# Head sums of four query and key tiles side by side, one inversion for four, and roots copied back over the heads' partitions on ScalarE's queue

## The reference

```python
def rmsnorm(x, g):                     # x: (..., heads, 64)
    x32 = x.astype(jnp.float32)
    y = x32 * lax.rsqrt(jnp.mean(x32 * x32, axis=-1, keepdims=True) + EPS)
    return (y * g.astype(jnp.float32)).astype(x.dtype)

def apply_rope(x, cos, sin):
    half = HEAD_DIM // 2
    x1, x2 = x[..., :half], x[..., half:]
    return jnp.concatenate([x1 * c - x2 * s, x2 * c + x1 * s], axis=-1)

q = apply_rope(rmsnorm(p_q.reshape(B, n, n_heads, HEAD_DIM), qg), *rope)
k = apply_rope(rmsnorm(p_k.reshape(B, n, n_kv,    HEAD_DIM), kg), *rope)
...
o = softmax(q k^T / 8, masks, sinks) v
```

## Time and profile before

| | |
|---|---|
| three runs, median (lowest, highest) | 3043.26 us (3042.82, 3045.39) |
| the profiled execution, its own time | 3041.93 us |
| its span, first to last instruction | 3039.8 us |
| TensorE matmuls busy | 2926.5 us, 96% |
| VectorE busy | 1115.6 us, 37% |
| ScalarE busy | 622.8 us, 20% |
| mean granted TensorE clock | 0.994 |

### The profile page before, as it was taken

One profiled execution on the slowest core, in us unless ns is written; L12 is line 12 of the kernel. 1 busy time (PEld: TensorE's weight loads), 2 busy tenths in 40 slices (PEclk: granted clock), 3 DMA queues, 4 the chain that ended last, 5 costly groups with the idle time before them and its releaser, 6 DMA issues.

```text
span 3039.8 us, 33448 instructions
## 1 busy us (share of the span) xinstructions
PE 2926.5 (96%) x13265; PEld 1464.3 (48%) x13265; DVE 1115.6 (37%) x1678; ACT 622.8 (20%) x1157; POOL 78.3 (3%) x92
## 2 busy tenths in 40 slices
PE   7999999999999999999999999999979998999999
PEld 4565655555555222222234655677433333334547
DVE  4764546566614000000147554334121110138352
ACT  3145530000002110101022453111011101021161
POOL 1000000000000001102000000000000000000000
PEclk9999999999999999999999999999989999999999
DMA  8230013443523899999971201223489999974300
GB/s 256 66 94 15 15 38 129 174 165 125 165 78 111 355 374 396 368 401 349 364 208 38 80 28 30 74 83 90 180 337 417 418 418 418 418 227 114 83 1 28
DMA packets 252321, 587.50 MB, mean 193 GB/s; under 512 B 64280, under 2 KB 143912, under 8 KB 231048
## 3 DMA queue, kind: packets, MB, share of 16 engines
q1 hardware_dynamic: 237072, 554.02, 49.4%
q0 software_dynamic: 7680, 22.62, 2.5%
q10 hardware_dynamic: 7416, 8.71, 1.2%
HBM read 561.44 MB, written 15.21 MB: 190 GB/s over the span
## 4 chain that ended last, share of the span: by engine, by line
PE 87%; DMA 7%; DVE 3%; issue 1%; ACT 1%; SPq 1%; ACTq 0%; DVEq 0%; POOL 0%; POOLq 0%
PE ps L1076 26%; PE ps L1527 10%; PE ps L1651 7%; PE ps L1539 5%; PE ps L1141 5%; PE ps L1096 5%; PE ps L1191 5%; PE ps L1367 3%; PE ps L1355 3%; PE ps L1401 3%; PE ps L1204 2%; PE ps L1588 2%; PE ps L1165 2%; DMA ring<-in_w_e_up 1%; DMA ring<-in_w_e_down 1%; PE ps L1341 1%
## 5 line engine op out<-in xcount | busy, mean ns | idle before, releaser
L1076 PE MATMUL ps<-hT,ring 128*128 128x512 f32 (+1 forms) x1696 | 604.5, 514 | 3.5 <-ACT hT L1889 3.4
L1076 PEld LDWEIGHTS ps<-hT,ring 128*128 128x128 f32 x1696 | 321.9, 191 | 276.0 <-issue 251.9
L1527 PE MATMUL ps<-ring,hT 128*64 128x512 f32 x992 | 235.9, 605 | 3.0 <-DMA ring<-in_w_e_up 3.0
L1141 PE MATMUL ps<-hT,ring 128*128 128x512 f32 (+1 forms) x448 | 181.5, 533 | 0.7 <-DVEq L1874 0.7
L1651 PE MATMUL ps<-ring,hT 128*64 128x512 f32 x640 | 157.6, 602 | 17.4 <-DMA ring<-in_w_e_down 10.0
L1889 ACT ACTIVATE prob<-prob,nms 128x768 f32<-128x768 f32 (+5 forms) x224 | 159.2, 711 | 14.9 <-DVE nms L2582 4.5
L1191 PE MATMUL ps<-merged,ring 128*128 128x512 f32 (+1 forms) x384 | 142.7, 526 | 3.1 <-issue 3.1
L1367 PE MATMUL ps<-con,prob 128*128 128x128 f32 x872 | 140.1, 283 | 3.5 <-DVE merged L2606 1.6
L1076 PE MATMUL ps<-obuf,ring 128*128 128x512 f32 (+1 forms) x384 | 142.1, 523 | 0.0
L1367 PEld LDWEIGHTS ps<-con,prob 128*128 128x128 f32 x872 | 96.4, 140 | 91.8 <-issue 78.8
L1889 ACT ACTIVATE prob<-ps 128x768 f32<-128x768 f32 (+2 forms) x55 | 36.7, 667 | 490.7 <-PE ps L1076 418.9
(11 more groups left out here) (368 smaller groups left out, 3675.1 us busy)
## 6 DMA issues: line engine op xcount, KB each, us to landing
ring<-in_w_e_gate SPq DMA_DIRECT2D x79, 1024.0 KB, 15.4
ring<-in_w_e_up SPq DMA_DIRECT2D x65, 1024.0 KB, 14.4
ring<-in_w_e_down SPq DMA_DIRECT2D x60, 1024.0 KB, 13.5
ring<-in_w_in SPq DMA_DIRECT2D x49, 1024.0 KB, 6.1
ring<-in_w_ada SPq DMA_DIRECT2D x48, 1024.0 KB, 6.7
merged<-in_w_e_up SPq DMA_DIRECT2D x25, 1024.0 KB, 14.8
merged<-in_w_e_down SPq DMA_DIRECT2D x19, 1024.0 KB, 12.6
merged<-in_w_e_gate SPq DMA_DIRECT2D x18, 1024.0 KB, 16.0
```

What stands on the lines that cost most here:

```text
L1076: mm = pe.matmul(ps[:, b + a:b + e], lhs[:, k, :], rhs[:, k, a:e], start=k == 0, stop=k == nk - 1)
L1141: mm = pe.matmul(ps[:, BANK[SIDE]:BANK[SIDE] + hi - lo], ring3(slot)[:, k, m % 2 * P:(m % 2 + 1) * P], h3[:, k, lo:hi], start=k == 0, stop ...
L1527: mm = pe.matmul(ps[e * CX:(e + 1) * CX, b + h * 512:b + (h + 1) * 512], lhs, second_weights(slot_of[sub], e, h), start=k == 0, stop=k == ...
```

## The change

Four tiles make a *quad* (in layers 0 and 1: four, four, two; in layer 2: four, four, four, one).

- Head sums: one matmul per tile and half still streams that tile's squares, but with only 32 columns of weights (16 columns of each head's ones), and the four tiles' matmuls go to four column groups of the array, at partitions 32r of the same PSUM bank. A tile's two sums thus lie on 32 partitions, 16 rows each.
- ScalarE takes the root and VectorE the inverse once for a quad (a 512-wide part, and a 256-wide one if there are wide tiles).
- A new job `spread`: ScalarE's queue starts one DMA per tile that reads the 32 rows of the inverse root, each four times, and writes 128 partitions (`inverse_roots`, in `merged` in layers 0 and 1, in `obuf` in layer 2).
- A new job `nrm` per tile on VectorE: tile times gain times inverse root. It waits until all copies of the quad have landed.
- `swap` is one job per quad that waits for the quad's last `nrm`; a DMA takes neighbouring tiles together, so that there are 12, 8 and 4 DMAs for the quads of a layer (40 before), and 8, 8, 8 and 4 in layer 2 (52 before). There are 10 or 13 DMAs of `spread` beside them. The rotations of a quad stand together; those of the last quad, two tiles, stand behind the second `S` in layers 0 and 1.
- The first value job of layer 2 now waits for the activations by itself.

```diff
-        roots = [rs, pr[:, 1, :]]
-        squares = [sq, pr[:, 2, :]]
+        roots = [rs, sq]
+        squares = [pr[:, r, :] for r in range(4)]
+        by_tile = merged[:].rearrange("p (r t) -> p r t", t=NT)
+        inverse_roots = [by_tile[:, 0:4, :]] * 2 + [obuf[:, 0:4 * NX].rearrange("p (r t) -> p r t", t=NX)]
+        turn_terms = [by_tile[:, 4:8, 0:NX]] * 2 + [obuf[:, 4 * NX:8 * NX].rearrange("p (r t) -> p r t", t=NX)]
...
         def pipelined(l, jobs):
-            order, sums, rots, swaps = [], [], [], []
...
+            tiles = [j[1:] for j in jobs if j[0] == "qk"]
+            order, waiting, made = [], [], 0
             for j in jobs:
                 order.append(j)
+                for stages in waiting:
+                    order += stages.pop(0)
+                waiting = [stages for stages in waiting if stages]
+                if j[0] != "qk":
+                    continue
+                made += 1
+                if made % 4 == 0 or made == len(tiles):
+                    n = (made - 1) // 4
+                    quad = tiles[4 * n:made]
+                    sums = [("hs", l, n), ("spread", l, n)]
+                    normed = [("nrm",) + t for t in quad] + [("swap", l, n)]
+                    rots = [("rot",) + t for t in quad]
+                    if made == len(tiles) and l < 2:
+                        for stages in waiting:
+                            order += sum(stages, [])
+                        waiting = [[sums + normed]]
+                        late = rots
+                    else:
+                        waiting.append([sums, normed, rots])
+            return order + late if l < 2 else order
...
+                    if j == ("v", 2, 0):
+                        need(h_ready, (2, "mix", KD - 1, 0))
...
-                    for a, e in halves(width(*j[1:])):
-                        mm = pe.matmul(ps[:, b + a:b + e], con[:, C_HEAD:C_HEAD + P], squares[hs_number[j] % 2][:, a:e],
-                                       start=True, stop=True)
+                    for a, e in halves(NT):
+                        for r, t in enumerate(quads[j]):
+                            if width(*t) >= e:
+                                mm = pe.matmul(ps[32 * r:32 * (r + 1), b + a:b + e], con[:, C_HEAD + HD - 16:C_HEAD + HD + 16],
+                                               squares[r][:, a:e], start=True, stop=True, tile_position=(0, 32 * r))
...
                 elif kind == "swap":
+                    quad = ("hs",) + j[1:]
+                    A.need(qn_ready, ("nrm",) + quads[quad][-1])
+                    if before_quad[quad]:
+                        A.need(q_ready, ("rot",) + quads[before_quad[quad]][-1])
+                    for a, e in kinds(quad):
+                        tiles = tiles_from(*quads[quad][a], e - a)
+                        for r in range(0, P, HD // 2):
+                            to, at = slice(r, r + HD // 2), r + HD // 2 if r % HD == 0 else r - HD // 2
+                            act.dma_start(turn_terms[l][to, a:e, :], tiles[at:at + HD // 2]).then_inc(s_swapped, 16)
+                elif kind == "spread":
+                    quad = ("hs",) + j[1:]
+                    A.need(inverted, quad)
+                    col = NT if hs_number[quad] % 2 == 0 else 0
+                    for r, t in enumerate(quads[quad]):
+                        w = width(*t)
+                        root_rows = bass.AP(sqrs, 32 * r * 2 * NT + col, [[2 * NT, 32], [0, P // 32], [1, w]])
+                        act.dma_start(inverse_roots[l][:, r, 0:w], root_rows).then_inc(s_spread, 16)
...
+                elif kind == "nrm":
+                    dve.wait_ge(s_spread, spread_at[quad_of[j[1:]]])
                     t = qk_dest(*j[1:])[:, 0:w]
-                    V.do(v.scalar_tensor_tensor(t, t, gain_col(*j[1:]), root[:, 0:w], ALU.mult, ALU.mult), qn_ready, j)
+                    V.do(v.scalar_tensor_tensor(t, t, gain_col(*j[1:]), inverse_roots[l][:, place_of[j[1:]], 0:w], ALU.mult, ALU.mult),
+                         qn_ready, j)
```

More of the change, by code:

```diff
@@ L514, in program, with kinds @@
         qsq_ready = event("head_square_ready", of("qk"))
[L515 removed]
+        inverted = event("head_roots_inverted", of("hs"))
+        qn_ready = event("head_normed", of("nrm"))
         q_ready = event("head_rotated", of("rot"))
[L517 to L519 removed]
+        s_spread = sem("head_roots_spread")
+        s_swapped = sem("head_halves_swapped")
+        quads, quad_of, place_of = {}, {}, {}
+        for n in range(3):
+            tiles = [j[1:] for j in PLAN[n] if j[0] == "qk"]
+            for at, t in enumerate(tiles):
+                quad_of[t], place_of[t] = ("hs", n, at // 4), at % 4
+                quads.setdefault(("hs", n, at // 4), []).append(t)
+        def kinds(quad):
+            out = []
+            for r, t in enumerate(quads[quad]):
+                if out and t[1][:-1] == quads[quad][r - 1][1][:-1] and t[1][-1].isdigit():
+                    out[-1][1] = r + 1
+                else:
+                    out.append([r, r + 1])
+            return out
+        swap_at, spread_at, before_quad = {}, {}, {}
+        swaps, spreads, quad_before = 0, 0, None
+        for j in of("hs"):
+            before_quad[j], quad_before = quad_before, j
+            swaps += len(kinds(j)) * P // (HD // 2) * 16
+            spreads += len(quads[j]) * 16
+            swap_at[j], spread_at[j] = swaps, spreads
         v_ready = event("values_ready", of("v"))
@@ L937, in width, with summed @@
             return NT if l == 0 or (l == 1 and name in ("ka", "kb")) else NX
+        def summed(quad):
+            wide = [r for r, t in enumerate(quads[quad]) if width(*t) == NT]
+            return [(slice(0, 32 * len(quads[quad])), 0, NX)] + ([(slice(32 * wide[0], 32 * (wide[-1] + 1)), NX, NT)] if wide else [])
         def halves(w):
```

95 lines of the change are left out of this document (43 added, 52 removed).

## The result

The changed kernel takes 3093.7 us (median of 4 runs, 3092.3 to 3095.3), the kernel before beside it 3044.3; the ratio is 1.0163, with a 95% interval of 1.0145 to 1.018. That is 49 us slower. The forecast was slower by 22 us, 3065, with a range up to 3081. The profiled execution took 3093.53 us, its span is 3091.6.

A forecast was written before the change was run, and what follows sets the result against it. TensorE was taken to bound the kernel (matmuls fill 96% of the span). Layer 0 +10.7, layer 1 +15.0, layer 2 -7.8 and clock +5 made +22.9 on 3041.93: 3065 us, range 3050 to 3081.

The forecast's parts named there:

- TensorE's work: Head sums of all three layers: four matmuls run abreast, saving 8.5, 5.9 and 7.3 us, 21.7 in all.
- The rival of head sums not abreast: Each quad's head sums cost 5.2 us (3.4 narrow), sum about +37, 3079 us; chance 0.04.
- The path, and the value copy behind it: Layers 0 and 1, head sums to first scores: TensorE waits 18.8 and 20.5 us, second value copy behind four swaps.
- I take 4.5, and 3.5: Landing of a quad's copies after the last issue: 4.5 us for a wide quad, 3.5 for 1 MB in layer 1.
- The rival with this mechanism: Copies bound by the 32 partitions they read: wide quad lands 11 to 12 us after issue, 3088 us; chance 0.10.
- landed 1.5 later: Layer 0's path: the second quad's eight swaps land 1.5 us after they are issued.
- a surcharge for weight loads in flight: Third quad's copies, with SP's weight loads in flight: landings raised from 3.8 and 2.7 to 6.0 and 5.0 us.
- ends ahead of TensorE up to a landing of 6.5 us: Layer 2's quads stay ahead of TensorE for landings up to 6.5 us, so layer 2 gains 7.8 us.
- Behind the first scores and the clock: Last rotations cost +1.4 us in each of layers 0 and 1; half clock behind two long waits costs +5.
- Given back: A later stretch bound by loads returns the 23 us of delay, leaving 3020 to 3025 us; chance 0.05.
- Cancelling landings near 1.5 us: Waits are smaller and cancel the savings, with no clock loss: 3043 to 3049 us; chance 0.08.

The follow-up runs named there:

- e1: Changed kernel with each inverse-root copy reading all 128 rows (64 where only 64 are filled) instead of 32 rows four times; values wrong: 3078.3 us.
- e8: Changed kernel with four-tile quads' copies reading 32 rows spread in steps of four, each four times; values wrong: 3073.9 us.
- e9: Changed kernel with four-tile quads' copies reading rows 0 to 63, each twice; values wrong: 3086.1 us.
- e4: Changed kernel with all copies and swaps issued by GpSimd's queue instead of ScalarE's, in the same order: 3065.4 us.
- e13: Changed kernel with layers 0 and 1 reordered (second swap behind third root), layer 2's order kept but its copies and swaps on GpSimd's queue: 3033.1 us.
- e10: Changed kernel with layers 0 and 1 reordered around the first scores, and layer 2's products and swap one tile later, rotations two and two: 3046.3 us.
- e2: Changed kernel without the inverse-root copies, the product taking the inverted root where it lies; values wrong: 3053.2 us.

## Why the forecast was right and wrong

**TensorE's work.** Right: a quad's head sums take 1.43 us wide (94.05 to 95.48 us) and 0.99 narrow against terms of 1.50 and 1.03. The rival of head sums not abreast falls.

**The path, and the value copy behind it.** Right as a chain: every step was found in the row where it was placed. Its sizes failed in two terms, so that the waits were 25.5 and 21.5 us (with 4.0 more ahead of the second) instead of 18.8 and 20.5.

*"I take 4.5, and 3.5": the landing of the copies.* From the first issue, 7.0 and 6.0 us were forecast for four wide and four narrow copies; 10.1 and 7.2 to 7.6 were measured where no load was in flight, 8.0 and 11.5 (narrow) where one was, and 9.9 for layer 1's first quad, which is half wide and was priced at 6.0. The rate was taken from ScalarE's queue as a whole, 4.1 us per MB, and the copies' source gives about half of what the same engines do with other rows (184 to 223 against 396 GB/s; e1, e8, e9). The rival with this mechanism had 0.10, and its landing was near, 10.1 us against 11 to 12. Its sum, 3088, was near by luck in part: layer 0 measured +20.1 with its clock against +23.5, layer 1 +23.8 against +27.5, and layer 2 +7.4 against -6, so that what it had too much in two layers stood against 13 us too little in the third. Its landing was argued away with the swaps, which also touch 32 partitions; but their time per MB came from a queue that was busy for 7.9% of the stretch, and no row showed it full.

*"landed 1.5 later": the swap of the second quad.* I gave the third quad's transfers a surcharge for weight loads in flight and the second quad's none; it landed 4.8 us after its last issue, 3.3 more than forecast. A load was in flight: from 160 to 164.6 us, when seven of the eight swaps were issued, SP's queue (q1) had 73% of the 16 engines and ScalarE's (q10) 5% (packets, MB, share):

```profile
q1 hardware_dynamic: 1028, 1.04, 73.0%
q10 hardware_dynamic: 45, 0.08, 4.7%
```

With the 3.1 us of the copies and 0.4 of issuing this is the 6.7 us by which layer 0's wait was longer than 18.8. But neither is its cause alone: e1 took the copies' part away and gained nothing in layer 0, because the third quad's copies landed at 191.7 to 191.9 us whether they were issued at 184.3 or at 180.8, with SP's loads in flight.

**Layer 2: "ends ahead of TensorE up to a landing of 6.5 us".** This step failed most, by 15.2 us. One landing was 7.3 us after its last issue (2842.20 to 2849.48) and the issuing itself 1.7 longer. But the bound itself was wrong too: the third quad's copies landed 3.7 us after their last issue (2883.29 to 2887.03), well under 6.5, and TensorE still stood 5.2 us at the last `silg`. I had followed the chain of the quads and not what stands behind the swap on ScalarE: squares of tiles that TensorE needs at the next head sums, and the `silg` jobs' own part. Faster copies clear it (e1, e8: 151.2 us, 7.5 less than before, where 7.8 were forecast), and so does another queue for them (e4, 152.2; e13, 153.0). A later place does not (e10: 160.2, one wait gone and two longer). So the cause is both together, a transfer of 7 to 11 us and a queue in which ScalarE's own work waits for it.

**Behind the first scores and the clock.** Right in size: 5.0 and 4.4 us against 3.9. The granted clock behind the long wait, and behind three short ones of 2.8, 4.5 and 5.2 us, in windows of the changed kernel (the clock is the third number from the end; 1.00 is the higher level, 2.4 GHz, 0.50 the lower, 1.2 GHz, and 0.56 a stretch that holds both):

```profile
197.00:200.00 3.00, 2.52 (x8) 1.27 (x8) 0.00 (x0) 1.58 (x2) 0.00 (x0) 0.50 0.20 47
...
203.00:206.00 3.00, 3.00 (x16) 1.67 (x16) 1.17 (x3) 1.46 (x4) 0.00 (x0) 1.00 0.00 0
...
213.00:216.00 3.00, 3.00 (x6) 1.14 (x6) 0.97 (x2) 2.64 (x5) 0.00 (x0) 0.56 0.01 3
...
2859.00:2862.00 3.00, 2.86 (x10) 1.04 (x11) 0.28 (x1) 0.83 (x3) 0.00 (x0) 0.50 1.04 277
...
2917.00:2921.00 4.00, 3.47 (x4) 1.51 (x5) 3.54 (x6) 0.77 (x2) 0.00 (x0) 0.50 0.00 0
```

The forecast reckoned with the two long waits alone, and in layers 0 and 1 that was nearly enough. In layer 2 each short wait cost again at the lower of the two levels: the value job behind it 15.73 us instead of 13.98, the `silg` projection 9.52 instead of 6.9. To the 9.7 us of waits there some 5 were added in this way.

**The other rivals.** Given back: no, no later stretch is shorter by more than 0.7 us. Cancelling landings near 1.5 us: no; even with no copies at all (e2) the time is 3053.

## What to carry to other kernels

A copy is priced by where its source rows lie as well as by its bytes: look at that before a rate is taken from another kind of transfer (the destination was all 128 partitions in each of these runs, so its part was not tested). A DMA issued by an engine that also computes puts everything behind it on that engine's row; when the wait ahead of an issue grows, either the order or the queue must change with it. And work done four at a time pays only if what needs the first results does not stand behind the last ones: here order and queue were worth 67.5 us, between 3093.7 and 3026.2, with the same arithmetic.

## What the runs showed of the hardware

- 32 neighbouring partitions as the source of a copy gave 184 to 223 GB/s in windows of 2 us, 64 neighbouring ones 203 to 209 (e9); 32 spread in steps of four gave 373 (e8) and all 128 gave 396 (e1).
- The time to issue a copy is not a constant: 0.67 us each in e1, where four land in 5.7 us, and 1.45 in the changed kernel, where they land in 10.1 (four issued in 2.69 and in 5.79 us).
- The clock's fall does not need a long wait: 2.8 us without matmuls, shortly after a longer one, was followed by a stretch with a granted clock of 0.56, and 4.5 and 5.2 us, each after more than 25 us of work, by 0.50.
- Two queues with sources in different halves moved a quad no faster than one (10.8 and 10.1 us, the second queue's copies moving some 2.4 us later; 250 GB/s with both under way against 223).
- Transfers of two queues at once share the engines unevenly: for 4.6 us a weight load had 73% of them and the swaps issued beside it 5%, and the swap landed 4.8 us after its last issue.
